# Rebuilding the first microseconds of a two-layer decoder trunk: norm row, positions, first mean square, fillers and the order of the first steps

## The reference, cut to what matters

```
x (256, 1024) f32, positions (256) int32
h    = x * rsqrt(mean(x*x) + 1e-6) * norm_mix_g[0]
proj = h @ w_in[0]                  # q, k, v, pooling, convolution and gate columns
ang  = positions[:, None] * inv_freq
q, k = rotated by cos(ang), sin(ang)
```

## Time and profile before

| | us |
|---|---|
| median of 3 runs | 1222.49 |
| the profiled execution's own time | 1222.39 |
| its span (first to last instruction) | 1220.6 |
| TensorE busy in the span | 1207.1 (99%) |
| VectorE, ScalarE, GpSimd busy | 897.7, 722.5, 108.0 |
| the first product of a tile starts at | 13.68 |
| the last product of tiles 0 and 1 starts at | 26.18 |

### The profile page before, as it was taken

How to read it: one execution, slowest core, us unless ns; L and a number is a source line. 1 busy time by engine, 2 the same in 40 slices (tenths; PEclk the granted TensorE clock), 3 DMA queues, 4 the chain that set the end, 5 groups by cost and what they waited for, 6 DMA issues and landing times.

```text
span 1220.6 us, 15437 instructions
## 1 busy us (share of the span) xinstructions
PE 1207.1 (99%) x6012; PEld 1002.6 (82%) x6012; DVE 897.7 (74%) x855; ACT 722.5 (59%) x681; POOL 108.0 (9%) x129
## 2 busy tenths in 40 slices
PE   9999999999999999999999999999999999999997
PEld 7997787788888888998778888888888888888876
DVE  5778755654544457767865788998888888888996
ACT  5447544534344346435643677777777777777765
POOL 3600000200000000340000000000010000000301
PEclk9999999999999999999999999999999999999999
DMA  9955454655555546554445499999999999999960
GB/s 299 324 173 167 146 183 160 228 186 186 192 181 201 175 170 223 191 173 173 139 172 175 146 350 371 389 373 386 383 386 382 387 381 386 383 390 377 393 274 35
DMA packets 152061, 317.03 MB, mean 260 GB/s; under 512 B 6258, under 2 KB 41330, under 8 KB 152003
## 3 DMA queue, kind: packets, MB, share of 16 engines
q1 hardware_dynamic: 147328, 302.27, 70.1%
q0 software_dynamic: 3968, 12.91, 2.9%
q10 hardware_dynamic: 706, 1.07, 0.3%
HBM read 310.47 MB, written 5.77 MB: 259 GB/s over the span
## 4 chain that ended last, share of the span: by engine, by line
PE 92%; DVE 4%; ACT 2%; issue 1%; POOLq 0%; POOL 0%; ACTq 0%; DVEq 0%
PE ps L1900 23%; PE ps L1629 17%; PE ps L1631 17%; PE ps L1630 17%; PE ps L1887 11%; DVE split L1009 2%; ACT split L636 1%; PE ps L1867 1%; PE ps L1645 1%; PE ps L1720 1%; PE ps L1749 1%; DVE hT L1045 1%; PE ps L1730 1%; PE ps L1666 1%; PE ps L1778 1%
## 5 line engine op out<-in xcount | busy, mean ns | idle before, releaser
L1009 DVE TENSOR_TENSOR split<-raw,split 128x2048 fp32r<-128x2048 f32 x279 | 638.9, 2294 | 205.4 <-ACT split L636 202.7
L636 ACT ACTIVATE split<-raw 128x2048 fp32r<-128x2048 f32 x279 | 534.5, 1916 | 252.3 <-PE ps L1631 181.5
L1900 PE MATMUL ps<-split,br 128*128 128x512 f32 x1344 | 317.4, 392 | 0.5 <-DVE split L1009 0.3
L1900 PEld LDWEIGHTS ps<-split,br 128*128 128x128 f32 x1344 | 249.5, 188 | 54.9 <-DVE split L1009 2.0
L1629 PE MATMUL ps<-split,hT 128*128 128x512 f32 (+1 forms) x600 | 235.0, 392 | 3.0 <-DVE hT L1045 1.7
L1631 PE MATMUL ps<-split,hT 128*128 128x512 f32 (+1 forms) x600 | 230.5, 384 | 0.0
L1630 PE MATMUL ps<-split,hT 128*128 128x512 f32 (+1 forms) x600 | 230.3, 384 | 0.0
L1887 PE MATMUL ps<-split,hT 128*128 128x512 f32 x672 | 159.6, 392 | 0.1
L1887 PEld LDWEIGHTS ps<-split,hT 128*128 128x128 f32 x672 | 124.8, 188 | 27.9 <-issue 1.6
L1629 PEld LDWEIGHTS ps<-split,hT 128*128 128x128 f32 x600 | 112.8, 188 | 31.1 <-issue 4.7
L1631 PEld LDWEIGHTS ps<-split,hT 128*128 128x128 f32 x600 | 112.7, 188 | 22.6
(11 more groups left out here) (278 smaller groups left out, 974.7 us busy)
## 6 DMA issues: line engine op xcount, KB each, us to landing
raw<-moe_w_gu_dram SPq DMA_DIRECT2D x96, 1024.0 KB
raw<-moe_w_down_dram SPq DMA_DIRECT2D x56, 1024.0 KB
raw<-w_in_dram SPq DMA_DIRECT2D x45, 1024.0 KB
raw<-ffn_w_gu_dram SPq DMA_DIRECT2D x28, 1024.0 KB
raw<-moe_w_gu_dram SPq DMA_DIRECT2D x32, 512.0 KB
raw<-ffn_w_down_dram SPq DMA_DIRECT2D x14, 1024.0 KB
raw<-w_branch_dram SPq DMA_DIRECT2D x12, 1024.0 KB
raw<-w_out_dram SPq DMA_DIRECT2D x8, 1024.0 KB
```

Of the source, the lines that this page charges most:

```text
L636: act.activation(buffer(t, 0), raw[:, t % RAW, :], ACT.Copy).then_inc(hi, 1)
L1009: dve.tensor_tensor(buffer(t, 1), raw[:, t % RAW, :], buffer(t, 0).bitcast(F32), ALU.subtract).then_inc(lo, 1)
L1900: ins = pe.matmul(ps[:, 5 if kind == "up" else 4, :], xe[:, sl, 4 * part + k, :], slot(t, sr, 512)[:, k, :], start=part + k + m == 0, stop ...
```

## The change

- The gain row of the first norm is no longer spread by TensorE. SyncE fetches it to all 128 partitions by a repeated read, in two halves of 256 KB: the first between the two blocks of x, the second behind the four pieces. The three DMAs of ScalarE are gone.
- Positions and frequencies are fetched by GpSimd, ahead of its 9 small DMAs and on their semaphore. So `small_in` counts 11 DMAs of layer 0, and `angles()` waits for `80 + 96`, which is 11 times 16. The other waits on `small_in` are raised by 32.
- The mean square of block 0 is one VectorE instruction (square, scale, sum, with EPS as the starting value of the sum). GpSimd's rstd of block 0 is then one instruction instead of two. Block 1 stays on ScalarE.
- TensorE's fillers: 7 at once, 4 when block 0 of x has landed, 1 when rstd is there, 2 behind the first transpose.
- The order of steps: only the first half block is transposed ahead of the products; the other three are transposed between products (`FIRST_TURNS`). The low part of tile 1 is made in four quarters (`second_lo`), and the products wait for each.

```diff
+FIRST_TURNS = ((0, 0, 2), (1, 0, 2), (1, 0, 3))
...
-            for b in range(NB):
-                sp.dma_start(X[:, b, :], x[0, b * P:(b + 1) * P, :]).then_inc(x_in[b], 16)
+            sp.dma_start(X[:, 0, :], x[0, 0:P, :]).then_inc(x_in[0], 16)
+            sp.dma_start(g_row[:, cols(0)], on_all(norm_mix_g[0:1, cols(0)])).then_inc(g_first, 16)
+            sp.dma_start(X[:, 1, :], x[0, P:2 * P, :]).then_inc(x_in[1], 16)
...
+                    sp.dma_start(g_row[:, cols(1)], on_all(norm_mix_g[0:1, cols(1)])).then_inc(g_second, 16)
...
+                    if n + b == 0:
+                        pool.wait_ge(first_ms, 1)
+                        pool.tensor_tensor(rstd[:, 0:1], ms[:, 0, 0:1], power[:, :], ALU.pow
+                                           ).then_inc(rstd_ready, 1)
+                        continue
...
                 if n == 0:
                     pool.wait_ge(y_ready, 2 * NB)
+                    pool.dma_start(pos_i[:, :], positions[0].rearrange("(b p) -> p b", p=P),
+                                   allow_slow_non_contiguous=True).then_inc(small_in, 16)
+                    pool.dma_start(freq[:, :], on_all(inv_freq)).then_inc(small_in, 16)
                     layer_loads(0)
...
-            act.dma_start(g_row[0:1, :], gains[0]).then_inc(g_first, 16)
-            act.dma_start(pos_i[:, :], positions[0].rearrange("(b p) -> p b", p=P),
-                          allow_slow_non_contiguous=True).then_inc(pos_in, 16)
-            act.dma_start(freq[:, :], on_all(inv_freq)).then_inc(pos_in, 16)
...
-            for b in range(NB):
-                act.wait_ge(x_in[b], 16)
-                act.activation(Y[:, b, :], X[:, b, :], ACT.Square, scale=D ** -0.5,
-                               accum_out=ms[:, b, 0:1]).then_inc(ms_ready, 2)
+            act.wait_ge(x_in[1], 16)
+            act.activation(Y[:, 1, :], X[:, 1, :], ACT.Square, scale=D ** -0.5,
+                           accum_out=ms[:, 1, 0:1]).then_inc(ms_ready, 2)
             piece_hi(0)
             turn_hi(0, (0,))
-            piece_hi(1)
+            for k in range(1, PIECES):
+                piece_hi(k)
             turn_hi(0, (1,))
-            piece_hi(2)
-            piece_hi(3)
             split_hi(1)
             turn_hi(0, (2, 3))
...
+            def second_lo(k):
+
+                cs = slice(k * 512, (k + 1) * 512)
+                dve.wait_ge(hi_ready, 2)
+                dve.tensor_tensor(buffer(1, 1)[:, cs], raw[:, 1, cs], buffer(1, 0)[:, cs].bitcast(F32),
+                                  ALU.subtract).then_inc(first_lo if k < PIECES - 1 else lo_ready, 1)
+
+            dve.wait_ge(x_in[0], 16)
+            dve.tensor_tensor_reduce(out=Y[:, 0, :], in0=X[:, 0, :], in1=X[:, 0, :], scale=1.0 / D, scalar=EPS,
+                                     op0=ALU.mult, op1=ALU.add, accum_out=ms[:, 0, 0:1]).then_inc(first_ms, 1)
             first_norm(0, 0)
-            first_norm(1, 0)
             piece_lo(0)
             turn_lo(0, (0,))
             piece_lo(1)
+            first_norm(1, 0)
+            piece_lo(2)
+            piece_lo(3)
             turn_lo(0, (1,))
-            piece_lo(2)
             first_norm(0, 1)
             first_norm(1, 1)
-            piece_lo(3)
-            split_lo(1)
-            turn_lo(0, (2, 3))
+            second_lo(0)
+            turn_lo(0, (2,))
+            for k in range(1, PIECES):
+                second_lo(k)
+            turn_lo(0, (3,))
 
             def angles():
 
-                dve.wait_ge(pos_in, 32)
+                dve.wait_ge(small_in, 80 + 96)
...
-            idle_work(6, 5, ones, ones)
-            pe.wait_ge(g_first, 16)
-            for nh in range(2):
-                pe.matmul(ps[:, 2 + nh, :], ones[0:1, :], g_row[0:1, cols(nh)], start=True, stop=True
-                          ).then_inc(g_spread, 1)
-            idle_work(8, 5, ones, ones)
+            idle_work(7, 5, ones, ones)
+            pe.wait_ge(x_in[0], 16)
+            idle_work(4, 5, ones, ones)
+            pe.wait_ge(rstd_ready, 1)
+            idle_work(1, 5, ones, ones)
             pe.wait_ge(consts, 10)
...
-            turn(0, Y, first_of, (0, 1))
+            turn(0, Y, first_of, (0,))
+            idle_work(2, 5, ones, ones)
...
-                    if b == 0 and (l or i):
+                    if l and b == 0:
                         pe.wait_ge(lo_ready, t0 + i + 1)
                     for k in range(4):
-                        if l + b + i == 0:
-                            if k == PIECES - 1:
-                                turn(0, Y, first_of, (2, 3))
-                            pe.wait_ge(*((first_lo, k + 1) if k < PIECES - 1 else (lo_ready, 1)))
+                        if l == 0 and (b, i, k) in FIRST_TURNS:
+                            turn(0, Y, first_of, (FIRST_TURNS.index((b, i, k)) + 1,))
+                        if l + b == 0:
+                            pe.wait_ge(*((first_lo, 3 * i + k + 1) if k < PIECES - 1 else (lo_ready, i + 1)))
```

More of the change, by code:

```diff
@@ L243, in trunk @@
         x_in = [sem(f"x_in{b}") for b in range(NB)]
-        pos_in, small_in, g_in = sem("pos_in"), sem("small_in"), sem("g_in")
+        small_in, g_in = sem("small_in"), sem("g_in")
         g_first = sem("g_first")
         y_last = [sem(f"y_last{i}") for i in range(2)]
-        g_spread = sem("g_spread")
+        g_second = sem("g_second")
+        first_ms = sem("first_ms")
         first_in = [sem(f"first_in{k}") for k in range(PIECES - 1)]
@@ L365, in trunk, with on_all @@
         block = ctx.enter_context(nc.Block())
+        def on_all(row):
+            return row.broadcast_to([P, row.shape[-1]])
         @block.sync
@@ L464, in trunk @@
                  final_norm_g.rearrange("(a n) -> a n", a=1)]
-        def on_all(row):
-            return row.broadcast_to([P, row.shape[-1]])
         @block.gpsimd
@@ L515, in rms @@
                 for b in range(NB):
-                    pool.wait_ge(ms_ready, 2 * (NB * n + b + 1))
+                    if n + b == 0:
[3 more added lines that the diff above has]
+                        continue
+                    pool.wait_ge(ms_ready, 2 * (NB * n + b))
                     if n == 0:
@@ L521, in rms @@
                                            ).then_inc(ms_plus, 1)
-                    pool.wait_ge(ms_plus, NB * n + b + 1)
+                    pool.wait_ge(ms_plus, NB * n + b)
                     pool.tensor_tensor(rstd[:, b:b + 1], rstd[:, b:b + 1], power[:, :], ALU.pow
@@ L674, in split_gate_hi @@
                 if i == 0:
-                    act.wait_ge(small_in, 48 + 96 * 2)
+                    act.wait_ge(small_in, 80 + 96 * 2)
                 act.wait_ge(landed[t % RAW], 32 * (t // RAW + 1))
@@ L1341, in first_norm @@
             def first_norm(b, nh):
-                dve.wait_ge(g_spread, 2)
+                dve.wait_ge(g_second if nh else g_first, 16)
                 dve.wait_ge(rstd_ready, b + 1)
-                dve.scalar_tensor_tensor(out=Y[:, b, cols(nh)], in0=X[:, b, cols(nh)],
-                                         scalar=rstd[:, b:b + 1], in1=ps[:, 2 + nh, :],
-                                         op0=ALU.mult, op1=ALU.mult).then_inc(y_ready, 1)
+                norm_half(0, b, nh)
             def piece_lo(k):
@@ L1392, in conv_taps @@
             def conv_taps(l, half):
-                dve.wait_ge(small_in, 48 + 96 * (l + 1))
+                dve.wait_ge(small_in, 80 + 96 * (l + 1))
                 dve.wait_ge(conv_v, 2 * l + half + 1)
@@ L2061, in _ @@
                 pe.wait_ge(pooled_ready, CH * (l + 1))
-                pe.wait_ge(small_in, 48 + 96 * (l + 1))
+                pe.wait_ge(small_in, 80 + 96 * (l + 1))
                 pe.wait_ge(conv_v, 2 * (l + 1))
```

## The result

The changed kernel takes 1231.37 us (median; 1230.46 to 1233.5 in 5 runs) against 1222.49: ratio 1.0078, 95% interval 1.0067 to 1.0089. It is slower by 8.9 us, 0.4 us beyond the top of the forecast range. The profiled execution took 1231.64, 9.25 more than the one of before (1222.39).

What follows compares the result with a forecast made beforehand. TensorE's queue was taken as the bound, with little cover over VectorE's chain. The start's 2.9 us gain is swallowed by stalls of 5.0 and 4.0 us, leaving 6.1 us later: 1222.4 + 6.1 = 1228.5 us, range 1222.5 to 1231.

Steps and rivals of the forecast that it cites:

- Change = L - 29.4: Rule for the whole kernel's change in us while L is above 26.5; forecast 6.1 us slower.
- L: Landing of GpSimd's last small DMA, g_col, for which VectorE's angles wait: forecast 35.5 us, range 33.5 to 36.5.
- The beginning alone gives 2.9 us: Products of tiles 0 and 1 end at 23.5 instead of 26.4 us; 4.2 with an early clock, about 1.5 with a late one.
- Landings: Start-up transfers: each half gain row costs 0.65 us at 408 GB/s, pieces land from 6.9 us, products begin at 9.4.
- I keep 12.8: TensorE's clock rises from its lower level to full at 12.8 us, although the change leaves TensorE more idle before that.
- Nothing waited for them but the norm: At the start, removing TensorE's gain-row matmuls and ScalarE's issues counts nothing by itself.
- the positions holding up the pieces: Positions in flight slow the pieces' transfers to 17 GB/s between 5 and 6 us; moving them gives back about 1.2 us.
- Room that is full: GpSimd's issue stops before the router or just behind it, where the count of contiguous runs reaches exactly 4096.
- Given back only when all in flight have landed: GpSimd's stopped list resumes only after the sinks land at 26.9 us, at 27.2, so g_col issues at 29.0.
- The cold TensorE: Rival, 10%: the stalls of 4 to 5 us before channel tiles 4 and 5 drop TensorE's clock; about 1230 us.
- A list that lands earlier: Rival, 13%: GpSimd issues and lands faster or room returns piecemeal; L between 27 and 31.8, time 1220.1 to 1224.8 us.
- A list without a stop: Rival, 9%: GpSimd's issue stop does not come, L is 27.8 or sooner; 1220.9 us, or 1219.5 below L = 26.5.

Runs made afterwards that it cites:

- kernel 1: The changed kernel with positions and frequencies counted on a semaphore of their own, for which the angles wait: 1221.39 us, ratio 1.0002 to the kernel before.
- kernel 2: The kernel before with only positions and frequencies moved to the head of GpSimd's list, on the shared semaphore: 1230.85 us, ratio 1.0079.
- kernel 9: The changed kernel with GpSimd's scratch room for DMA descriptors 6144 bytes instead of 4096: 1232.26 us, ratio 1.0086.
- 10, room 4608: The changed kernel with GpSimd's scratch room for DMA descriptors 4608 bytes instead of 4096: 1232.07 us in one run.
- Kernel 4: As kernel 1, with 10 fillers instead of 2 behind the first transposed half: 1220.08 us, ratio 0.9985 to the kernel before.
- Kernel 3: As kernel 1, with block 1 of x issued ahead of the first half of the gain row: 1221.97 us, ratio 0.9999.
- kernel 8: As Kernel 4, but gain row as before (4 KB by ScalarE, spread by TensorE), fillers 6, 2, 1 and 5: 1222.47 us, ratio 1.0007.
- kernel 11: As kernel 6, with 10 fillers instead of 2 behind the first transposed half: 1220.56 us, ratio 0.9989 to the kernel before.
- kernel 6: The changed kernel, shared semaphore kept, with router, g_router and g_col issued after layer 0's pooling; angles wait for eight DMAs: 1222.65 us, ratio 1.0006.
- kernel 7: The kernel before with 2 instead of 8 fillers behind the spreading of the gain row: 1220.98 us, ratio 0.9995.
- kernel 5: The kernel before with positions and frequencies issued by GpSimd ahead of its list, on a semaphore of their own: 1222.42 us, ratio 1.0004.

## Why the prediction was right, and where it was not

**What bounds the end, the wait, and who stands behind it: right.** The wait for all 11 DMAs costs the whole loss (kernel 1 takes it away, kernel 2 makes it alone). "Change = L - 29.4" holds in every profiled execution with the stall, with the start of the angles, which is g_col's landing there, put in for L:

| kernel | angles start | 1222.39 + start - 29.4 | that execution |
|---|---|---|---|
| changed | 38.53 | 1231.52 | 1231.64 |
| 2, before with the move | 34.05 | 1227.04 | 1226.95 |
| 9, room 6144 | 38.38 | 1231.37 | 1231.32 |
| 10, room 4608 | 39.06 | 1232.05 | 1232.07 |

**The step that failed is L**, forecast 35.5 (33.5 to 36.5) and measured 38.5. By its own terms: the list's start 18.17 instead of 15.7, +2.5; from there to the sinks' issue 5.28 instead of 5.2; the stop 6.18 where the forecast's times leave 5.7, +0.5; router and g_router 1.76 instead of 1.8; g_col's latency 6.54 instead of 6.5. Together 3.0. So 2.5 of the 2.9 us by which the time missed (1231.37 against 1228.5) are the late start of the list, that is the step "**The beginning alone gives 2.9 us**": its end of the norms (15.6) was carried into L. L's upper bound of 36.5 let the start be no later than forecast, though the text itself named a case in which the clock rose 3 us later. That was a range too narrow, not an unknown mechanism. Kernel 4, with the same late landings but a full clock, starts its list at 16.71. So up to 1.5 of the 2.5 us are the clock, and 1.0 or more the landings.

**Why the beginning gave nothing before the wait.** Tile 3 ended at 38.4, as before (38.35), where 35.4 was forecast. Three terms failed:
- *Landings.* The half gain row was priced by its bytes at 408 GB/s, 0.65 us. It took some 2 us, in which the engines moved 104 and 176 GB/s; block 1 of x came 2.1 us later than taken, the pair for the products at 11.4 instead of 9.4. Kernel 3 shows the slow stretch moving with the row, kernel 8 shows it gone without the row.
- *The clock.* "I keep 12.8" for its rise, with no reason given for keeping it: it was up when the first half was transposed (four transposes in 0.63 us at 7.80), fell while TensorE stood for 2.52 us ahead of the first product, and rose near 17. Kernel 4 against 1 prices that at 1.3 us, kernel 11 against 6 at 2.1. (Kernels 1 and 6 have the same beginning, yet their clocks rose near 15 and near 17.)
- *The chain before.* "Nothing waited for them but the norm", of the gain-row matmuls and the fillers, was wrong for the kernel before. Its chain of work that ended last, followed through the first microseconds, is this:

```profile
3.99 3.71 PE ps L1991 x4
7.70 3.71 PE ps L1666 x16
11.41 0.87 PE ps L1645 x4
```

The spread and the eight fillers stand in it one behind the other, and kernel 7 starts its transposes at 8.08 without six of them. The prediction shows no row of this view. And "the positions holding up the pieces" (1.2 us back) was right as a reading of 17 GB/s, up to the frequencies, which moved with them, but kernel 5 shows that no time hung on it: the pieces were not what the products waited for.

A slip of the working changes little: 39 matmuls between 17.39 and 26.18 start in 38 steps, 0.231 us each and not 0.226.

**The stop: right in place, and in mechanism but for one point; 0.5 us short in size.** "Room that is full", the count of 4096 with the router, and the place before it are all borne out by kernels 9 and 10. "Given back only when all in flight have landed" needs a narrower form. In kernel 1 positions and frequencies had their own semaphore, and the router waited only 0.81 us, until just behind the landing of the frequencies. g_router then waited for the router. From the DMA issues of kernel 1:

```profile
router_sb<-moe_router_dram POOLq DMA_DIRECT2D x1, 32.0 KB, 7.3
...
freq<-inv_freq_dram POOLq DMA_DIRECT2D x1, 16.0 KB, 5.3
```

Issued at 18.84, the frequencies land at 24.1 (the router goes at 24.49); the router lands at 24.49 + 7.3 = 31.8 (g_router goes at 32.15). Kernels 4 and 5 show the same pair of waits, 0.89 and 6.30 us, 0.84 and 6.71. With one shared semaphore the stop lasted until the last of its DMAs had landed, though positions and frequencies had landed some 5 us before. So room came back per semaphore; no run varied this further, so how it is kept stays open.

**The cold TensorE: right that a drop in the first stall is hidden.** The drop fell in the first stall and the second hid it, so it was no cause of the miss. The 1230 given for this rival had a drop in the second stall, which did not come; that it lies nearest to the time is luck. The Trainium skill, TensorE: Matmul & The Clock Gate, section Why this matters for your kernels, warns of idle gaps of TensorE in mid-kernel, which bring its clock down; the trace agrees, with 1.00 at 38 to 40 us and 0.50 from 42 on, in a gap of 4.99 us.

**The rivals.** A list that lands earlier falls: nothing on GpSimd went faster for VectorE's standing idle (the router's issue 0.91 us against 0.90, g_col's landing 6.5 both times). The Trainium skill, DMA: Bandwidth & Descriptors, section on the anatomy of one DMA on the GpSimd path, gives about 2.0 us fixed. The trace disagrees for this stretch, where g_col took 6.54. Issued behind the pooling, at 65.4 to 67.3 in kernel 6, the three DMAs took 2.9 us each, with the engines moving 85 GB/s in 65:68 instead of some 350: this fits a price that hangs on what else is under way. By the skill's 2.0 us the sinks too would land early, and the forecast's own steps then give, as an estimate, L = 20.9 + 2.0 + 0.3 + 1.8 + 2.0 = 27.0, not the 31 of the prediction. A list without a stop, the rival on the other side, was made in kernels 6 and 11 by taking three DMAs out of it: with the clock late it gives 1222.65, with it early 1220.56, not 1219.5. No run has all 11 without a stop.

## What to carry to other kernels

A wait on a semaphore that many DMAs share is a wait for the last of them: before an early consumer is put on it, work out when the last one lands, stops of the issuing queue included, or give the early ones a semaphore or a count of their own (that alone turned 1231.4 into 1221.4). When a start-up step is rebuilt, read the chain of waits for what it really hangs on, fillers among it; fillers that keep the clock up pay only where TensorE would stand anyway (kernel 4), and at half clock each one too many lengthens the path (0.47 us each in the profile of before). Price a transfer by its access pattern, not its bytes: a row read repeatedly for all partitions took about three times the time of its bytes at the start of this kernel.

## What the runs showed of the hardware, unexpected

- A repeated read of one row at 104 GB/s, later 176, with DMA shares of 0.95 and 0.98. In the other profiles with this order the rates are about the same (98 to 115, then 168 to 207), but the shares lie between 0.33 and 0.75: slow landing is shown, busy engines are not. The second half row, issued behind the pieces, left no such stretch: 9:10 moved 410 GB/s at 1.06. Why the first is slow and the second not was not tried.
- GpSimd's issue stop moves one DMA on when the room goes from 4096 to 4608 and again at 6144, lasts 6 to 7 us each time, and is shortened to 0.81 to 0.89 us for one DMA by giving the first two another semaphore.
- The clock of the first 17 us depends on a few fillers: two against ten behind the first transposed half decide between half and full from 12 to 14 us. With two, the rise came between 14.0 (kernel 9) and 17.05 (changed). The column of the clock has to be read with the distance of the matmuls: it shows 1.00 up to the first change, in kernel 9 for 12 to 14 us too, where products start 0.43 us apart (12.14, 12.57, 12.99), and in the kernel before until 12 us, with fillers of 0.47. The runs of the kernel before fall into two groups, 1219.1 to 1220.4 and, most of them, near 1222.4; that this is an early and a late rise of the clock is argued from kernel 2's profile (four transposes in 0.63 us at 8.04, half clock nowhere in its products of tiles 0 and 1, fastest of its runs), not shown for the kernel before.
